# HGRN and GLA level scores: one product for two heads, keys stacked, late queries laid out block-wise with zeros, one pick a level

## The chip, the cores and the metric

The kernel runs on one core of a Trainium2 chip. The metric is the time of one execution on the device in microseconds. The kernel before has a median of 2030.61 us over three runs.

## The reference, cut to what matters

Two layers are computed on 512 tokens of width 1024, all in float32. Each layer has a mixer with four branches, a cross attention and a squared-ReLU MLP. Two of the mixer's branches, HGRN and GLA, are gated linear recurrences with four heads each, worked out in chunks of 64 tokens:

```
def chunk_gated_linear(q, k, v, log_g):
    qc, kc, vc, gc = [jnp.moveaxis(to_chunks(t), 2, 0) for t in (q, k, v, log_g)]
    g_cum = jnp.cumsum(gc, axis=-2)
    def step(s_st, inp):
        ...
        diff = gb[:, :, :, None, :] - gb[:, :, None, :, :]
        decay = jnp.exp(jnp.where(causal[:, :, None], diff, -jnp.inf))
        att = jnp.einsum('bhtk,bhsk,bhtsk->bhts', qb, kb, decay)
        o = o_inter + jnp.einsum('bhts,bhsv->bhtv', att, vb)
```

The head width `dk` is 64 in HGRN and 32 in GLA. The change is in how `att` is computed. The decay between a query t and a key s depends on the channel, so it can't be put on the finished score.

## The kernel before, in words

All activations lie with channels on partitions and the 512 tokens on the free axis. HGRN's queries and keys fill two tiles of 128x512 (heads 0 and 1 in the first, 2 and 3 in the second; `m.J` is 2), GLA's fill one (four heads of 32 partitions; `m.J` is 1). There are 8 chunks (`NCH`) of 64 tokens (`CH`).

The scores of a chunk are made in seven levels. Level 0 is the diagonal s = t. For the levels 1 to 6, with widths w = 32, 16, 8, 4, 2, 1 (`LEVELS`), a chunk is cut into pairs of blocks of w tokens: the keys are those of the early block of a pair, the queries those of the late one, and both are decayed to the border between the blocks. One level is a chain over three engines and back:

- VectorE: `level_diff` subtracts the cumulated log gates from those at the border, for the early and for the late half (two tensor_tensor into `m.E`).
- ScalarE: `level_exp` takes the exponential of `m.E`, and counts up `hg_exp` or `gl_exp`.
- VectorE: `level_mul` multiplies `m.E` into the keys (early half) and into the queries (late half). Both results go to the same tile `m.X`. It counts up `x_ready` (`hg_x`, `gl_x`).
- TensorE: `scores` waits for `x_ready` and runs 32 products, one for each of the 4 heads and 8 chunks. Stationary are 64 keys (64 or 32 partitions), moving are 32 late queries. The chunk's parity picks the lower or the upper 64 partitions of the result. It counts up `lev_done`.
- VectorE: `pick` copies, under a mask, what belongs to this level from PSUM (the banks `M[0]` to `M[3]`) into `m.att` (copy_predicated: 2 a level in HGRN, 4 in GLA), and counts up `picked`.

Each engine works through its own list, written out by hand. TensorE's list is mostly large products: `gemm` and `parts` multiply by weights that come in 680 units of 2 x 256 columns through a ring of 9. For each unit, SyncE's queue loads `w_raw`, ScalarE rounds it to `w_hi` (`feed`, line 1190), and GpSimd subtracts to give `w_lo` (lines 598 and 599), which counts up `split_ready`. TensorE waits for that before a unit. The level scores stand between these blocks: `scores(hg, 3)`, say, stands between the products of the blocks `r_g` and `gate3_0`, and `scores(gl, 6)` ahead of `branch3_2`.

ScalarE feeds units only at certain places of its own list. The five units that start with that of `branch3_2` are fed in `gate(3, 2)`, behind four tanh that wait for `conv(0)` to `conv(3)` on VectorE. VectorE's list there is `level_mul(gl, 3)`, `level_mul(gl, 4)`, two `level_diff`, `pick(gl, 3)`, `merge(3, 0)`, `conv(0)`, `conv(1)`, `pick(gl, 4)`, `level_mul(gl, 5)`, `level_mul(gl, 6)`, `last_decay`, `conv(2)`, `pick(gl, 5)`, `decayed`, `conv(3)`.

Nearly every VectorE and TensorE operation is recorded under the line of a helper: 605 is every matmul, 1660 tensor_tensor, 1669 scalar_tensor_tensor.

Of the kernel before, what the change touches and what calls it, by code (L numbers as in the profile page):

```python
# [19 lines left out]
CH = 64  # L20
# [48 lines left out]
def shape_constants():  # L69
# [27 lines left out]
    put("parity", np.stack([(r // 16) % 2 == 0, (r // 16) % 2 == 1], 1).astype(np.float32))  # L97
    m = np.zeros((P, len(LEVELS), CH), np.int32)
# [54 lines left out]
def is_last(u):  # L153
# [24 lines left out]
    th_used=38, hg_diff=13, s5_prm=1, hg_picked=14, hg_x=6, hg_kdecay_ready=1, hg_state_ready=2, y_act=8, y_ready=8,  # L178
    gl_diff=13, gl_picked=28, gl_x=6, mlstm_cv_ready=4, mlstm_v1=3, gl_kdecay_ready=1, gl_state_ready=2,
# [7 lines left out]
def build(nc, ins, out):  # L187
# [7 lines left out]
    with ctx:  # L195
# [64 lines left out]
        M = [ctx.enter_context(nc.psum_tensor(f"mix{b}", [P, 512], F32)) for b in range(4)]  # L260
# [41 lines left out]
        class Mixer:  # L302


            def __init__(self, pre, tiles, dk, q, k, v, g, gr, e, xx, att, kt, state, o, sq, gscale, oscale, norm):
# [6 lines left out]
                self.X = [Rf(xx + tiles * i, tiles) for i in range(2)]  # L312
# [14 lines left out]
            def score_bank(self, level, h):  # L327
                return M[2 * (level % 2) + h % 2] if self.J == 2 else M[h]

            def score_cols(self, h):  # L330
                return (h // 2) * 256 if self.J == 2 else 0

            def slot(self, h):

                return (h % 2) * 2 + h // 2 if self.J == 2 else h

        hg = Mixer("hg", 2, HD, 4, 2, 6, 0, 8, 10, 14, 18, 20, 22, 10, 12, 1.0, 0.5, "hgrn_norm")
        gl = Mixer("gl", 1, GDK, 26, 27, 28, 32, 30, 10, 12, 14, 20, 22, 12, 10, 1.0 / 16.0, GDK ** -0.5, "gla_norm")
# [264 lines left out]
        def _(pe):  # L603
# [81 lines left out]
            def scores(m, l):  # L685
# [9 lines left out]
                if m.J == 2 and l >= 2:  # L695
                    pe.wait_ge(*of_layer(m.picked, 2 * (l - 1)))
                if m.J == 1 and l >= 1:
                    pe.wait_ge(*of_layer(m.picked, 4 * l))
                kk, qq = (m.K, m.Q) if l == 0 else (m.X[l % 2], m.X[l % 2])

                n = CH if l == 0 else CH // 2
                for h in range(4):
                    rows = slice(m.dk * (h % m.per), m.dk * (h % m.per) + m.dk)
                    base = (h // m.per) * SEQ
                    for c in range(NCH):
                        at_ = m.score_cols(h) + (c // 2) * CH
                        tok = slice(base + c * CH, base + c * CH + CH)
                        late = qq[rows, tok]
                        if l:
                            late = late.rearrange("p (n a c) -> p n a c", a=2, c=LEVELS[l])[:, :, 1, :]  # L710
                        i = mm(m.score_bank(l, h)[64 * (c % 2):64 * (c % 2) + 64, at_:at_ + n], kk[rows, tok], late)
                i.then_inc(m.lev_done, 1)

            def decayed_keys(m):

                pe.wait_ge(*of_layer(m.kd_ready, 1))
                pe.wait_ge(*of_layer(m.picked, 2 * 7 if m.J == 2 else 4 * 7))
# [18 lines left out]
            def outputs(m):  # L736
# [441 lines left out]
        def _(act):  # L1178
# [162 lines left out]
            for L in range(DEPTH):  # L1341
# [25 lines left out]
                do(act.activation(hg.X[1], hg.X[1], ACT.Abs))  # L1367
                do(act.activation(hg.X[1], hg.X[1], ACT.Exp, scale=-1.0))
                do(act.activation(hg.X[1], hg.X[1], ACT.Ln, bias=one), hg.gate_in)
# [287 lines left out]
        def _(dve):  # L1657
# [81 lines left out]
            def level_mul(m, l):  # L1739
# [5 lines left out]
                e, xx, k, q = v(m.E[l % 2]), v(m.X[l % 2]), v(m.K), v(m.Q)  # L1745
                tt(xx[:, :, 0, :], e[:, :, 0, :], k[:, :, 0, :], ALU.mult)
                tt(xx[:, :, 1, :], e[:, :, 1, :], q[:, :, 1, :], ALU.mult, m.x_ready)

            def pick(m, l):

                dve.wait_ge(*of_layer(m.lev_done, l + 1))
                nb = 2 if m.J == 2 else 4
                w = 1024 // nb
                for b in range(nb):
                    bank = m.score_bank(l, b)
                    r = lambda ap: ap.rearrange("p (n c) -> p n c", c=CH)
                    if l == 0:
                        do(dve.copy_predicated(r(m.att[:, b * w:(b + 1) * w]), bc(LM[:, l, :], 1, w // CH), r(bank[:, 0:w])), m.picked)
                        continue
                    dst = m.att[:, b * w:(b + 1) * w].rearrange("p (n s a c) -> p n s a c", n=w // CH, a=2, c=LEVELS[l])[:, :, :, 1, :]  # L1760
                    src = r(bank[:, 0:w])[:, :, 0:CH // 2].rearrange("p n (s c) -> p n s c", c=LEVELS[l])
                    mask = LM[:, l, :].rearrange("p (s a c) -> p s a c", a=2, c=LEVELS[l])[:, :, 1, :]
                    do(dve.copy_predicated(dst, bc(mask, 1, w // CH), src), m.picked)
# [625 lines left out]
```

## Time and profile before

| what | us |
|---|---|
| the three runs | 2030.36, 2030.61, 2031.58 |
| span of the profiled execution, first to last instruction | 2028.1 |
| TensorE matmuls busy | 1999.2 |
| VectorE busy | 961.2 |
| ScalarE busy | 913.2 |
| GpSimd busy | 1062.4 |

The runs lie 2.3 to 3.5 us above the span of the profile, which leaves out what comes ahead of the first and behind the last instruction. A float32 product appears as two matmul records, so that a block of 32 products has 64 of them. A matmul's own duration contains the way through the array. How fast products follow each other is seen from their starts.

### The profile page before, as it was taken

The numbers are of one execution on the slowest core, as the hardware profiler recorded it, in microseconds if no ns is written. First come the engines' busy times: TensorE is split into PE (matmuls) and PEld (weight loads), VectorE is DVE, ScalarE is ACT, GpSimd is POOL, SyncE is SP. The second block draws the span as 40 slices with busy tenths as digits, with TensorE's granted clock in tenths as the row PEclk, the third lists the DMA queues.
The fourth block names the chain that finished last, engine by engine and source line by source line (L and its number), as shares of the span: only waits on it lengthen the run. The fifth ranks groups of instructions, "written<-read, shape, count | busy, mean of one in ns | idle before, by whom it ended". The sixth has DMA issues, their size and how long they took to land. (4 is left out here: it accounts for less than half of the span.)

```text
span 2028.1 us, 32997 instructions
## 1 busy us (share of the span) xinstructions
PE 1999.2 (99%) x12983; PEld 1667.4 (82%) x12983; DVE 961.2 (47%) x1448; ACT 913.2 (45%) x1561; POOL 1062.4 (52%) x1364
## 2 busy tenths in 40 slices
PE   7999999999999999999999999999999999999998
PEld 7788888878998888888897888878788888888887
DVE  6665799845234321211257567997541532211112
ACT  6744554334545542423356536243454544433323
POOL 4564453746744555546466435457377355546451
PEclk9999999999999999999999999999999999999999
DMA  5422233323432333333333232323334233333332
GB/s 176 113 76 76 74 84 86 93 89 94 144 101 68 95 98 99 94 99 97 96 85 90 73 80 79 79 76 97 99 121 129 69 90 97 95 98 99 94 99 73
DMA packets 202678, 191.24 MB, mean 94 GB/s; under 512 B 25658, under 2 KB 200220, under 8 KB 202140
## 3 DMA queue, kind: packets, MB, share of 16 engines
q1 hardware_dynamic: 202524, 189.15, 32.1%
q8 instruction: 102, 1.67, 0.3%
q14 instruction: 52, 0.43, 0.1%
HBM read 184.90 MB, written 3.15 MB: 93 GB/s over the span
## 5 line engine op out<-in xcount | busy, mean ns | idle before, releaser
L598 POOL TENSOR_TENSOR w_lo<-w_raw,w_hi 128x256 fp32r<-128x256 f32 (+1 forms) x680 | 554.2, 815 | 938.2 <-ACT w_hi L1190 937.9
L605 PE MATMUL gemm<-work_split,w_hi 128*128 128x512 f32 (+1 forms) x2048 | 599.6, 377 | 1.8 <-POOL w_lo L599 1.7
L605 PE MATMUL gemm<-h_hi,w_hi 128*128 128x512 f32 (+1 forms) x1456 | 575.9, 396 | 2.3 <-POOL w_lo L599 2.3
L605 PE MATMUL gemm<-h_lo,w_hi 128*128 128x512 f32 (+1 forms) x1456 | 567.3, 390 | 0.0
L605 PE MATMUL gemm<-h_hi,w_lo 128*128 128x512 f32 (+1 forms) x1456 | 567.0, 389 | 0.0
L599 POOL TENSOR_TENSOR w_lo<-w_raw,w_hi 128x256 fp32r<-128x256 f32 (+1 forms) x680 | 557.9, 821 | 0.0
L1190 ACT ACTIVATE w_hi<-w_raw 128x512 fp32r<-128x512 f32 (+1 forms) x680 | 384.0, 619 | 237.7 <-DMA w_raw<-in_mlp_w_dram 185.9
L605 PEld LDWEIGHTS gemm<-work_split,w_hi 128*128 128x128 f32 x2048 | 375.3, 188 | 73.3 <-issue 2.5
L605 PE MATMUL gemm<-work_split,w_lo 128*128 128x512 f32 (+1 forms) x1024 | 384.9, 376 | 0.0
L605 PEld LDWEIGHTS gemm<-h_hi,w_hi 128*128 128x128 f32 (+1 forms) x1456 | 272.7, 187 | 66.0 <-issue 4.2
L605 PEld LDWEIGHTS gemm<-h_hi,w_lo 128*128 128x128 f32 (+1 forms) x1456 | 272.7, 187 | 58.4
L605 PEld LDWEIGHTS gemm<-h_lo,w_hi 128*128 128x128 f32 (+1 forms) x1456 | 272.8, 187 | 57.3 <-issue 1.9
L1660 DVE TENSOR_TENSOR x_t<-x_t,gemm 128x512 f32<-128x512 f32 x96 | 66.0, 688 | 364.0 <-PE gemm L605 363.1
L605 PEld LDWEIGHTS gemm<-work_split,w_lo 128*128 128x128 f32 x1024 | 192.8, 188 | 34.9
L1660 DVE TENSOR_TENSOR work<-work 128x512 f32<-128x512 f32 (+5 forms) x154 | 129.0, 837 | 43.4 <-ACT work L1281 29.3
L1669 DVE SCALAR_TENSOR_TENSOR gate_t<-gemm,work 128x512 f32<-128x512 f32 x64 | 44.3, 692 | 184.3 <-PE gemm L605 167.4
L1635 ACT ACTIVATE gate_t<-gate_t 128x512 f32<-128x512 f32 x64 | 40.5, 632 | 191.0 <-DVE gate_t L1669 191.0
L605 PEld LDWEIGHTS mix<-work 64*64 64x64 f32 (+5 forms) x3776 | 102.1, 130 | 27.2 <-issue 23.8
L605 PE MATMUL mix<-work 64*64 64x64 f32 (+8 forms) x3776 | 121.4, 231 | 0.0
L1275 ACT ACTIVATE gate_t<-gemm 128x512 f32<-128x512 f32 x52 | 31.1, 598 | 131.6 <-PE gemm L605 121.8
L605 PE MATMUL gemm<-w_hi,work_split 128*128 128x256 f32 x384 | 84.8, 288 | 4.3 <-DVE merged_split L1669 2.8
L1669 DVE SCALAR_TENSOR_TENSOR work_split<-gate_t,work_split 128x512 fp32r<-128x512 f32 x64 | 44.7, 699 | 89.0 <-ACT work_split L1636 89.0
(302 smaller groups left out, 1743.7 us busy)
## 6 DMA issues: line engine op xcount, KB each, us to landing
w_raw<-in_mlp_w_dram SPq DMA_DIRECT2D x256, 256.0 KB, 2.7
w_raw<-in_w_in_dram SPq DMA_DIRECT2D x224, 256.0 KB, 2.8
w_raw<-in_xattn_w_kv_dram SPq DMA_DIRECT2D x64, 256.0 KB, 2.8
w_raw<-in_w_branch_dram SPq DMA_DIRECT2D x32, 256.0 KB, 2.7
w_raw<-in_w_out_dram SPq DMA_DIRECT2D x32, 256.0 KB, 2.7
w_raw<-in_xattn_w_q_dram SPq DMA_DIRECT2D x32, 256.0 KB, 2.8
w_raw<-in_xattn_w_o_dram SPq DMA_DIRECT2D x32, 256.0 KB, 2.7
work<-in_x_dram SPq DMA_DIRECT2D x4, 512.0 KB, 6.5
```

Source lines behind the costliest of these rows:

```text
L598: pool.tensor_tensor(lo[:, 0:half], raw[:, 0:half], hi[:, 0:half].bitcast(F32), ALU.subtract)
L599: pool.tensor_tensor(lo[:, half:], raw[:, half:], hi[:, half:].bitcast(F32), ALU.subtract).then_inc(split_ready, 1)
L605: return pe.matmul(o, w, a, start=start, stop=stop, skip_group_check=True)
L1190: act.activation(hi, raw, ACT.Copy).then_inc(split_hi, 1)
L1275: do(act.activation(t[:, b, :], G[s][b][:, :], ACT.Tanh, scale=0.5), th_ready)
L1635: do(act.activation(UPX[1], UPX[0], ACT.Square), up_a)
L1660: do(dve.tensor_tensor(o, a, b, op), s)
L1669: do(dve.scalar_tensor_tensor(out=o, in0=a, scalar=sc, in1=b, op0=op0, op1=op1), s)
```

## The change

Both levels' operands get tiles of their own: `m.early` holds the decayed keys, `m.late` the decayed queries. `m.late` has, for each chunk, 64 columns: 32 late queries times the constant `in_pair` of head 0 of a pair (1 on that head's partitions, 0 on the other's), then the same 32 times that of head 1. One product of stacked keys (128 partitions in HGRN, 64 in GLA) with these 64 columns gives the scores of two heads beside each other. So `scores` has 16 products a level for level 1 to 6 where there were 32. `pick` becomes one copy_predicated of 512 columns a level from level 1 on; for GLA it reads over two banks. `level_mul` becomes three operations: one for the keys and, for each head of a pair, one scalar_tensor_tensor for the queries. In HGRN's levels 1 and 2 the one for the keys takes all 1024 columns. Level 0 stays as it was but for where it writes in `m.att`. The banks go round differently: HGRN uses one of four a level, GLA two of four, and TensorE's waits for `picked` reach further back.

```diff
@@ class Mixer
-            def score_bank(self, level, h):
-                return M[2 * (level % 2) + h % 2] if self.J == 2 else M[h]
+            def score_bank(self, level):
+                return (level + 1) % 4 if self.J == 2 else 2 - 2 * (level % 2)
@@ scores
-                if m.J == 2 and l >= 2:
-                    pe.wait_ge(*of_layer(m.picked, 2 * (l - 1)))
-                if m.J == 1 and l >= 1:
-                    pe.wait_ge(*of_layer(m.picked, 4 * l))
-                kk, qq = (m.K, m.Q) if l == 0 else (m.X[l % 2], m.X[l % 2])
-
-                n = CH if l == 0 else CH // 2
-                for h in range(4):
-                    rows = slice(m.dk * (h % m.per), m.dk * (h % m.per) + m.dk)
-                    base = (h // m.per) * SEQ
...
+                elif m.J == 2:
+                    if l >= 3:
+                        pe.wait_ge(*of_layer(m.picked, max(2, l - 2)))
+                    for j in range(2):
+                        for c in range(NCH):
+                            o = M[m.score_bank(l)][64 * (c % 2):64 * (c % 2) + 64, (j * 4 + c // 2) * CH:(j * 4 + c // 2 + 1) * CH]
+                            i = mm(o, m.early[l % 2][:, (j * NCH + c) * CH:(j * NCH + c + 1) * CH], m.late[l % 2][:, (j * NCH + c) * CH:(j * NCH + c + 1) * CH])
+                else:
+                    pe.wait_ge(*of_layer(m.picked, max(4, l + 2)))
                     for c in range(NCH):
...
+                        for p in range(2):
+                            rows = slice(64 * p, 64 * p + 64)
+                            o = M[m.score_bank(l) + p][64 * (c % 2):64 * (c % 2) + 64, (c // 2) * P:(c // 2 + 1) * P]
+                            i = mm(o.rearrange("p (h x) -> p h x", h=2)[:, :, 0:CH // 2], m.early[l % 2][rows, c * CH:(c + 1) * CH],
+                                   m.late[l % 2][rows, c * CH:(c + 1) * CH])
@@ level_mul
-                e, xx, k, q = v(m.E[l % 2]), v(m.X[l % 2]), v(m.K), v(m.Q)
-                tt(xx[:, :, 0, :], e[:, :, 0, :], k[:, :, 0, :], ALU.mult)
-                tt(xx[:, :, 1, :], e[:, :, 1, :], q[:, :, 1, :], ALU.mult, m.x_ready)
+                e, k, q = v(m.E[l % 2]), v(m.K), v(m.Q)
+                if m.J == 2 and l <= 2:
+                    tt(m.early[l % 2], m.E[l % 2], m.K, ALU.mult)
+                else:
+                    tt(v(m.early[l % 2])[:, :, 0, :], e[:, :, 0, :], k[:, :, 0, :], ALU.mult)
+                of_chunk = lambda ap: ap.rearrange("p (n s) c -> p n s c", s=CH // (2 * w))
+                late = m.late[l % 2].rearrange("p (n h s c) -> p n h s c", h=2, s=CH // (2 * w), c=w)
+                for h in range(2):
+                    stt(late[:, :, h, :, :], of_chunk(e[:, :, 1, :]), m.in_pair[:, h:h + 1], of_chunk(q[:, :, 1, :]), ALU.mult, ALU.mult,
+                        m.x_ready if h else None)
@@ pick, levels 1 to 6
+                dst = m.att.rearrange("p (n s a c) -> p n s a c", n=16, a=2, c=w)[:, :, :, 1, :]
+                if m.J == 2:
+                    src = M[m.score_bank(l)].rearrange("p (n c) -> p n c", n=16)
+                else:
+                    b = m.score_bank(l)
+                    src = MIX[:, 512 * b:512 * b + 1024].rearrange("p (n c) -> p n c", n=16)[:, :, 0:CH // 2]
+                mask = LM[:, l, :].rearrange("p (s a c) -> p s a c", a=2, c=w)[:, :, 1, :]
+                do(dve.copy_predicated(dst, bc(mask, 1, 16), src.rearrange("p n (s c) -> p n s c", c=w)), m.picked)
```

VectorE, from `pick(hg, 1)` to `level_mul(hg, 3)` and `pick(hg, 2)`, before:

```order
L1763 COPY_PREDICATED work<-masks_sb,mix 128x8x32 [waits hg_scores,vector_steps]
L1763 COPY_PREDICATED work<-masks_sb,mix 128x8x32 [waits hg_picked]
L1660 TENSOR_TENSOR work<-work 128x128x4 [waits hg_x,hg_picked]
L1660 TENSOR_TENSOR work<-work 128x128x4 [waits hg_diff]
L1669 SCALAR_TENSOR_TENSOR work<-gate_t,gemm 128x512 [waits th_ready,hg_diff]
L1669 SCALAR_TENSOR_TENSOR work<-gate_t,gemm 128x512 [waits th_used,th_ready]
L1660 TENSOR_TENSOR work<-work 128x64x8 [waits th_used,hg_scores,hg_exp]
L1660 TENSOR_TENSOR work<-work 128x64x8 [waits vector_steps]
L1763 COPY_PREDICATED work<-masks_sb,mix 128x16x16 [waits hg_scores,hg_x]
L1763 COPY_PREDICATED work<-masks_sb,mix 128x16x16 [waits hg_picked]
```

and the same stretch of VectorE now:

```order
L1785 COPY_PREDICATED work<-masks_sb,mix 128x16x32 [waits hg_scores,vector_steps]
L1669 TENSOR_TENSOR work<-work 128x128x4 [waits hg_x,hg_picked]
L1669 TENSOR_TENSOR work<-work 128x128x4 [waits hg_diff]
L1678 SCALAR_TENSOR_TENSOR work<-gate_t,gemm 128x512 [waits th_ready,hg_diff]
L1678 SCALAR_TENSOR_TENSOR work<-gate_t,gemm 128x512 [waits th_used,th_ready]
L1669 TENSOR_TENSOR work<-work 128x64x8 [waits th_used,hg_scores,hg_exp]
L1678 SCALAR_TENSOR_TENSOR work<-work,consts_sb 128x16x32 [waits vector_steps] x2
L1785 COPY_PREDICATED work<-masks_sb,mix 128x32x16 [waits hg_scores,hg_x]
```

The order of the steps is the same; each pick is one row instead of two, and the second tensor_tensor of a `level_mul` has become two scalar_tensor_tensor. Ahead of this stretch, `level_mul(hg, 1)` and `level_mul(hg, 2)` on VectorE are now:

```order
L1669 TENSOR_TENSOR work<-work 128x1024 [waits hg_exp,pro_tensor,hg_picked]
L1678 SCALAR_TENSOR_TENSOR work<-work,consts_sb 128x16x32 [waits vector_steps] x2
L1669 TENSOR_TENSOR work<-work 128x1024 [waits hg_exp,hg_x]
L1678 SCALAR_TENSOR_TENSOR work<-work,consts_sb 128x16x32 [waits vector_steps] x2
L1669 TENSOR_TENSOR work<-work 128x64x8 [waits hg_x]
```

where there were four tensor_tensor of 512 columns; the last row is the first of `level_diff(hg, 3)`, which follows as before.

## Rows read from the trace of the kernel before

**Rows 1.** The page: busy us (share); a group's busy us, mean ns of one.

```profile
PE 1999.2 (99%) x12983; PEld 1667.4 (82%) x12983; DVE 961.2 (47%) x1448; ACT 913.2 (45%) x1561; POOL 1062.4 (52%) x1364
...
L605 PE MATMUL mix<-work 64*64 64x64 f32 (+8 forms) x3776 | 121.4, 231 | 0.0
```

**Rows 2.** TensorE's waits: total us, times, longest us.

```profile
PE gemm L605 <- POOL w_lo L599: 5.5, 6, 1.5
```

**Rows 3.** TensorE's timeline around `scores(hg, 3)`, layer 1, then layer 2: start, us.

```profile
113.43 0.39 PE L605 MATMUL gemm<-h_hi,w_lo 128*128 128x512 f32 x1
113.75 1.46 PE L605 MATMUL mix<-work 64*64 64x32 f32 x64
...
1109.65 1.46 PE L605 MATMUL mix<-work 64*64 64x32 f32 x64
```

**Rows 4.** TensorE's timeline: blocks of other shapes.

```profile
150.06 2.79 PE L605 MATMUL mix<-work 64*64 64x64 f32 x120
...
360.05 0.86 PE L605 MATMUL mix<-work 128*32 128x32 f32 x64
...
366.52 3.71 PE L605 MATMUL mix<-work 128*64 128x128 f32 x64
```

**Rows 5.** TensorE's timeline: `scores(hg, 1)`, `scores(gl, 1)`, `scores(gl, 3)`, first of `branch3_2`.

```profile
99.64 1.46 PE L605 MATMUL mix<-work 64*64 64x32 f32 x64
...
170.53 1.45 PE L605 MATMUL mix<-work 32*64 32x32 f32 x64
...
190.21 1.45 PE L605 MATMUL mix<-work 32*64 32x32 f32 x64
...
220.90 0.50 PE L605 MATMUL gemm<-work_split,w_hi 128*128 128x512 f32 x1
```

**Rows 6.** VectorE's timeline in HGRN's levels.

```profile
96.69 5.58 DVE L1660 TENSOR_TENSOR work<-work 128x512 f32<-128x512 f32 x6 [5.14 <-ACT work L1281]
...
105.13 0.93 DVE L1763 COPY_PREDICATED work<-masks_sb,mix 128x256 f32<-128x256 int32 x2
...
109.79 1.84 DVE L1660 TENSOR_TENSOR work<-work 128x512 f32<-128x512 f32 x2 [0.22 <-DVE work L1669]
...
129.43 1.52 DVE L1763 COPY_PREDICATED work<-masks_sb,mix 128x256 f32<-128x256 int32 x2 [1.68 <-PE mix L605]
```

**Rows 7.** GpSimd's timeline: its first and last operation beside that stretch.

```profile
98.42 1.01 POOL L598 TENSOR_TENSOR w_lo<-w_raw,w_hi 128x256 fp32r<-128x256 f32 x1 [8.43 <-ACT w_hi L1190]
...
106.29 1.17 POOL L599 TENSOR_TENSOR w_lo<-w_raw,w_hi 128x256 fp32r<-128x256 f32 x1
```

**Rows 8.** VectorE's timeline, single operations: prices by width, alone and beside GpSimd.

```profile
97.42 0.69 DVE L1660 TENSOR_TENSOR work<-work 128x512 f32<-128x512 f32 x1
...
110.52 1.12 DVE L1660 TENSOR_TENSOR work<-work 128x512 f32<-128x512 f32 x1
...
126.11 1.64 DVE L1660 TENSOR_TENSOR work<-work 128x1024 f32<-128x1024 f32 x1
...
130.99 1.23 DVE L1660 TENSOR_TENSOR work<-work 128x1024 f32<-128x1024 f32 x1
...
158.15 0.75 DVE L1669 SCALAR_TENSOR_TENSOR work<-work,params_all 128x512 f32<-128x512 f32 x1 [9.33 <-ACT work L1308]
```

**Rows 9.** VectorE's timeline in GLA's levels.

```profile
168.88 0.85 DVE L1660 TENSOR_TENSOR work<-work 128x256 f32<-128x256 f32 x1
...
189.04 3.65 DVE L1660 TENSOR_TENSOR work<-work 128x256 f32<-128x256 f32 x8 [5.72 <-ACT work L1281]
192.72 1.30 DVE L1763 COPY_PREDICATED work<-masks_sb,mix 128x128 f32<-128x128 int32 x4
...
211.32 1.90 DVE L1763 COPY_PREDICATED work<-masks_sb,mix 128x128 f32<-128x128 int32 x4 [0.17 <-PE mix L605]
```

**Rows 10.** The unit of `branch3_2`: ScalarE's last tanh, GpSimd's second half.

```profile
216.97 0.63 ACT L1449 ACTIVATE work<-work 128x512 f32<-128x512 f32 x1 [5.11 <-DVE work L1669]
...
219.05 1.17 POOL L599 TENSOR_TENSOR w_lo<-w_raw,w_hi 128x256 fp32r<-128x256 f32 x1
```

More of the change, by code:

```diff
@@ L97, in shape_constants @@
     put("parity", np.stack([(r // 16) % 2 == 0, (r // 16) % 2 == 1], 1).astype(np.float32))
+    put("in_pair", np.stack([(r // w) % 2 == n for w in (64, 32) for n in range(2)], 1).astype(np.float32))
     m = np.zeros((P, len(LEVELS), CH), np.int32)
@@ L259, in build @@
         G = [[ctx.enter_context(nc.psum_tensor(f"gemm{s}{b}", [P, 512], F32)) for b in range(2)] for s in range(2)]
-        M = [ctx.enter_context(nc.psum_tensor(f"mix{b}", [P, 512], F32)) for b in range(4)]
+        MIX = ctx.enter_context(nc.psum_tensor("mix", [P, 4 * 512], F32))
+        M = [MIX[:, 512 * b:512 * b + 512] for b in range(4)]
         def bc(ap, axis, n):
@@ L302, in build, with __init__ @@
         class Mixer:
-            def __init__(self, pre, tiles, dk, q, k, v, g, gr, e, xx, att, kt, state, o, sq, gscale, oscale, norm):
+            def __init__(self, pre, tiles, dk, q, k, v, g, gr, e, xx, early, att, kt, state, o, sq, gscale, oscale, norm):
                 self.pre, self.J, self.dk, self.gscale, self.oscale, self.norm = pre, tiles, dk, gscale, oscale, norm
@@ L311, in __init__ @@
                 self.E = [Rf(e + tiles * i, tiles) for i in range(2)]
-                self.X = [Rf(xx + tiles * i, tiles) for i in range(2)]
+                self.late = [Rf(xx + tiles * i, tiles) for i in range(2)]
+                self.early = [Rf(early + 2 * i, tiles) for i in range(2)]
+                self.in_pair = const("in_pair")[:, 0:2] if tiles == 2 else const("in_pair")[:, 2:4]
                 self.att = Rf(att, 2)
@@ L725, in state_in @@
                 pe.wait_ge(*of_layer(m.kt_ready, m.J))
+                pe.wait_ge(*of_layer(m.picked, 8 if m.J == 2 else 10))
                 pe.wait_ge(*of_layer(values_ready, VALUES_AT[m.pre]))
@@ L1366, in _ @@
                        hg.kq_ready if j else None)
-                do(act.activation(hg.X[1], hg.X[1], ACT.Abs))
-                do(act.activation(hg.X[1], hg.X[1], ACT.Exp, scale=-1.0))
-                do(act.activation(hg.X[1], hg.X[1], ACT.Ln, bias=one), hg.gate_in)
+                do(act.activation(hg.late[1], hg.late[1], ACT.Abs))
+                do(act.activation(hg.late[1], hg.late[1], ACT.Exp, scale=-1.0))
+                do(act.activation(hg.late[1], hg.late[1], ACT.Ln, bias=one), hg.gate_in)
                 feed_past("r_q")
@@ L1753, in pick @@
[L1753 to L1763, printed above, removed]
+                if l == 0:
+                    att = m.att.rearrange("p (j t h c) -> p j t h c", j=2, t=TT, h=2)
+                    for b in range(2 if m.J == 2 else 4):
+                        if m.J == 2:
+                            dst, n = att[:, :, :, b, :].rearrange("p j t c -> p (j t) c"), 8
+                        else:
+                            dst, n = att[:, b // 2, :, b % 2, :], 4
+                        do(dve.copy_predicated(dst, bc(LM[:, l, :], 1, n), M[b][:, 0:n * CH].rearrange("p (n c) -> p n c", c=CH)), m.picked)
+                    return
```

43 lines of the change are left out of this document (24 added, 19 removed).

## The prediction

> **What bounds the kernel now.** The page comes first: TensorE is busy for 1999.2 us of the span, 99% of it, and no other engine for more than 52% [rows 1]. Its waits come next: the longest group is 5.5 us in six waits for `w_lo` [rows 2]. So the kernel is bound by what TensorE has to do in its own order, and a level's scores are part of that. The third view is TensorE's timeline at a score block. The last large product starts at 113.43, the block at 113.75, after the 0.32 that every such block shows. The block lasts 1.46 for 64 records (32 products, two records each), in the second layer just the same [rows 3]. Without the last record's own 0.23 [rows 1], the starts take 1.23 us, 20 ns a record. GLA's blocks last 1.45 [rows 5]. There are 24 such blocks (six levels, two branches, two layers) and none of them waits for VectorE. The fourth view is VectorE's timeline there, which tells how near the operands come. All depends on it, because the change gives VectorE more to do ahead of the blocks.
>
> **TensorE, removed.** A block now has 32 records instead of 64. No row has a 128*64 product with 64 moving columns. The same stationary shape with 128 columns starts a record every (3.71 - 0.23) / 63 = 55.2 ns [rows 4]. If columns set it, 64 of them take 27.6 ns, and 31 intervals with 0.05 for the start give 0.90 us. If they don't, it is 55.2 x 31 = 1.71. The quickest small shape, 128*32 with 32 columns, starts one every (0.86 - 0.23) / 63 = 10 ns [rows 4], which gives 0.31. I take 0.90, since that shape differs in one number only: HGRN saves 0.33 a level, 4.0 us in 12. For GLA (64*64, 64 columns, row halves and column halves in turn) the nearest row is the block of 120 records in 2.79 [rows 4], 21.5 ns a record, of which about half go round four quarters of the array and the rest round two. At 27 ns for the latter, the former take about 16 ns, so 31 intervals take 0.50 (between 0.31 and 0.67). GLA, whose block takes 1.22 now, saves 0.72 a level, 8.6 us in 12. Together that is 12.6 us of TensorE's work.
>
> The Trainium skill ("TensorE: Matmul & The Clock Gate", section "Back-to-back issue gap") says that 1 to 64 moving columns cost the same, some 25 ns a matmul. The trace has 20 ns a record here, and by this rule 32 records take 0.8 in both branches and save 0.43 a level, 10.3 us in all.
>
> **VectorE, added.** Prices: a tensor_tensor of 512 columns takes 0.69 alone and 1.12 while GpSimd works on `w_lo`; one of 1024 takes 1.23 alone and 1.64 beside it. A scalar_tensor_tensor of 512 with a per-partition factor takes 0.75 alone [rows 8], and I take 1.12 beside GpSimd. Between two operations lie 0.035. A pick costs 0.465 for 256 columns and 0.325 for 128, so 0.74 for 512; in the levels w = 2 and 1 it is 0.76 for 256 and 0.475 for 128, so 1.36 for 512 [rows 6, 9].
>
> **HGRN.** VectorE works without a break from 96.69 to 109.79 [rows 6], with GpSimd beside it from 98.42 to 107.46 in eight operations [rows 7]. Before, `hg_x` for level 1 came at 98.11, 1.53 ahead of the block at 99.64 [rows 5, 8]. Now it comes at 96.69 + 1.265 + 0.785 + 1.12 = 99.86: the block waits about 0.3. Level 2's multiplications end at 99.90 + 1.675 + 1.155 + 1.12 = 103.85 instead of about 99.98 (four tensor_tensor from 96.69, three alone and one beside GpSimd). From there to `level_mul(hg, 3)` there were 9.81 us. The pick gives back 0.19, and I take off 0.5, since `level_diff(hg, 4)` now falls into GpSimd's pause. So it starts at 112.95 and takes 0.725 + 1.155 + 1.12 = 3.0: `hg_x` comes at 115.95, where it came at 111.63 for a block at 113.75 [rows 3, 6]. TensorE would be there at 113.75 + 0.3 - 2 x 0.33 = 113.4 and waits 2.7 (with 0.1 from the count to the first product). Behind the waiting product stand the large ones of `gate3_0` and all of TensorE's list, so the wait is paid in full. What is late next: level 4 needs a pick (0.77), `level_diff(hg, 5)` and three multiplications, at most 0.77 + 2.3 + 3.4 = 6.5 after level 3, and the next block comes 7.05 - 0.33 = 6.7 after it (7.05 is half of the way from 99.64 to 113.75). That is just in time, and so is level 5. The later operations fall into pauses that VectorE had (1.68 ahead of the pick at 129.43 [rows 6]). ScalarE feeds units some us later there; none of today's waits for `w_lo` is long (six in all, the longest 1.5 [rows 2]). In a layer HGRN gives 6 x 0.33 - 3.0 = -1.0 us.
>
> The bounds of this wait: with the added operations alone on the port they cost 1.4 + 1.4 + 0.8 - 0.2 = 3.4 instead of 4.3, and the two waits are 2.1. With GpSimd beside each of them they cost 6.0, and the waits are 4.7.
>
> **GLA.** A `level_mul` grows from 0.91 to 0.465 + 2 x 0.515 = 1.50. Level 1's second operation ended at 168.88 + 0.85 = 169.73 [rows 9], ahead of a block at 170.53 [rows 5]. Now the end is at about 170.6: a wait of 0.15. Level 2 has more room. Level 3's multiplications start at 189.04, when ScalarE's exponential is ready, and ended 0.91 later for a block at 190.21 [rows 5, 9]; now they end at 190.50, a wait of 0.35. For the levels 4 to 6 the operands are early by more than that.
>
> The costlier wait is at `branch3_2`. ScalarE's tanh at 216.97 waited for `conv(3)` on VectorE. Only behind it does ScalarE feed the unit of `branch3_2`, and GpSimd ends its second half at 219.05 + 1.17 = 220.22 [rows 10], for products that began at 220.90 [rows 5]. That is 0.7 to spare on one chain: VectorE from 189.04 on, which has hardly a pause up to `conv(3)`. Along this chain the change adds four `level_mul` (4 x 0.585 = 2.34), takes off 1.34 - 0.77 = 0.57 at each of `pick(gl, 3)` and `pick(gl, 4)` and 1.93 - 1.36 = 0.57 at `pick(gl, 5)`, and uses up the 0.17 that VectorE stood idle there for TensorE [rows 9]. The sum is +0.46: the unit is ready at 220.7. But TensorE, with four blocks shortened, would be there at 220.90 - 4 x 0.72 + 0.35 = 218.4. It waits 2.4, and from the start of level 3 to `branch3_2` it gains 0.15 instead of 2.88. Afterwards units come in time, and both engines' lists are as before. In a layer GLA gives 2 x 0.72 - 0.15 + 0.15 = +1.44 us.
>
> Bounds: with the factors' operations at tensor_tensor's price (0.43), the chain is not longer at all and the gain is 0.6 instead of 0.15. With one operation of each `level_mul` beside GpSimd (+0.4 each) it is 2.1 longer and 1.5 are lost.
>
> Costless: four more constant columns, the wait of `level_mul(hg, 1)` for the prologue's transposes (long done by then), other addresses in `m.att`, and the waits for `picked`, which reach further back.
>
> **The sum.** 2 x (1.44 - 1.0) = 0.9 us off the span of 2028.1, so 2027.2. The median of the runs is 2.5 above the span: 2029.7.
>
> **Rivals.** (A) The forecast: most of the 12.6 us turns into waits. 0.55; its own range is 2026.9 (both lower bounds: -0.1 and +1.9 a layer) to 2032.5.
> (B) The waits don't come and TensorE's saving is the result: 2030.6 - 12.6 = 2018.0. For it: 99% busy and no wait for VectorE today [rows 1, 2]. Against it: margins of 1.53, 2.1, 0.8, 0.26 and 0.7 us against more than 4 us of added work. 0.08.
> (C) Only one of the two long waits comes. Without `branch3_2`'s, 2 x 2.4 more are gained: 2024.9. Without HGRN's, 2 x 3.0: 2023.7. Both sums rest on several prices, so 0.12.
> (D) Slower: GpSimd stands beside each added operation. The added work ahead of `hg_x` for level 3 is then 6.0 instead of 4.3, and the waits in HGRN come to 4.7; in GLA the chain grows by 2.1. That is a layer at -2.7 - 0.2, 5.8 in both: 2036.4. It decides once the two chains together are longer by 2.6 a layer than I take. For it: GpSimd follows ScalarE's feeding, which VectorE's delay also moves. Against it: GpSimd has a fixed number of operations and its pauses stay. 0.12, of which most is over 2034.7.
> (E) VectorE and GpSimd shut each other out for a whole operation: 0.69 + 0.73 = 1.42 instead of the 1.12 of [rows 8], 0.3 more for each of four added operations, 1.2 a layer: 2032.0. 0.05. The Trainium skill states this rule ("SBUF — State Buffer", section "Terms": the port pair is locked for the whole instruction and the loser "fully blocks"). The trace speaks against the full price here.
> (F) A block is quicker or slower than taken. In levels 1 to 3 of HGRN and 3 to 6 of GLA a wait swallows it, so it moves the time by under 2 us: 0.08.
>
> **How the numbers follow.** 0.2% is 4.1 us, about what a measurement can tell from no change. Faster means under 2026.5: B, C and a little of A and F, 0.22. Slower means over 2034.7: most of D, 0.12. Within it 0.66. The range takes in C from below and part of D: 2023.5 to 2035.0.
>
> **What the profile will show.** HGRN's blocks at about 0.9 and GLA's at 0.5 from first to last start; TensorE waiting for VectorE about 2.7 at `scores(hg, 3)` and 0.3 at `scores(hg, 1)`; about 2.4 for GpSimd's `w_lo` at `branch3_2`; TensorE's busy time down by about 12.6 and its waits up by 12. If waits at these places are missing, B or C holds; if the one in HGRN is over 4, D.

## The result, and the profile after

The changed kernel takes 2034.24 us (median of 20 runs, 2032.16 to 2036.66). The kernel before takes 2031.12 in 20 runs (2029.70 to 2032.49). The ratio is 1.0017, with a 95% interval of 1.0011 to 1.0023: slower by some 3 us, where the forecast was 0.9 us faster. The profiled execution has a span of 2032.3 us; its whole time is 1.8 us more.

Two lines of the page, as in [rows 1]:

```profile
PE 1993.9 (98%) x12215; PEld 1660.3 (82%) x12215; DVE 976.3 (48%) x1424; ACT 912.6 (45%) x1561; POOL 1067.3 (53%) x1364
...
L606 PE MATMUL mix<-work 64*64 64x64 f32 (+7 forms) x3008 | 109.1, 235 | 5.9 <-DVE work L1678 5.9
```

And TensorE's waits, as in [rows 2] (total us, times, longest us):

```profile
PE gemm L606 <- POOL w_lo L600: 9.2, 7, 2.4
PE mix L606 <- DVE work L1678: 5.9, 6, 2.4
```

The waits that were forecast have come: 5.9 us for VectorE's scalar_tensor_tensor (L1678) in six waits, where there were none, and 9.2 us for `w_lo` instead of 5.5. But TensorE's busy time fell by 5.3 us only, while its group of small products fell by 12.3 (from 121.4 [rows 1]). So the rest of its work, which the change doesn't touch, is busy for 7 us more. That is the first sign. TensorE's timeline of blocks gives their sizes (start, us, and in brackets the idle time before it). The rows are `scores(hg, 1)`, `(hg, 3)` and `(hg, 4)` in layer 1, `scores(gl, 1)` and `(gl, 3)`, then `(hg, 3)` and `(hg, 4)` in layer 2:

```profile
100.56 1.15 PE L606 MATMUL mix<-work 128*64 128x64 f32 x32 [0.30 <-DVE work L1678]
...
116.50 1.52 PE L606 MATMUL mix<-work 128*64 128x64 f32 x32 [2.37 <-DVE work L1678]
124.79 1.15 PE L606 MATMUL mix<-work 128*64 128x64 f32 x32
...
173.70 0.69 PE L606 MATMUL mix<-work 64*64 64x64 f32 x32
192.23 0.69 PE L606 MATMUL mix<-work 64*64 64x64 f32 x32 [0.28 <-DVE work L1678]
...
1115.33 1.15 PE L606 MATMUL mix<-work 128*64 128x64 f32 x32 [2.38 <-DVE work L1678]
1122.07 1.15 PE L606 MATMUL mix<-work 128*64 128x64 f32 x32
```

A block of HGRN takes 1.15 and one of GLA 0.69, where each took 1.46 or 1.45 [rows 3, 5]. The two blocks `(hg, 3)` had waited equally long, 2.37 and 2.38. Yet from the one to `(hg, 4)` it is 8.29 us in layer 1 and 6.74 in layer 2, with the same instructions between. The large products in between show why. Timeline of TensorE in layer 1, directly behind the block:

```profile
117.96 0.80 PE L606 MATMUL gemm<-h_hi,w_hi 128*128 128x512 f32 x1
118.55 0.63 PE L606 MATMUL gemm<-h_lo,w_hi 128*128 128x512 f32 x1
118.98 0.63 PE L606 MATMUL gemm<-h_hi,w_lo 128*128 128x512 f32 x1
...
119.83 0.63 PE L606 MATMUL gemm<-h_lo,w_hi 128*128 128x512 f32 x1
120.26 0.51 PE L606 MATMUL gemm<-h_hi,w_lo 128*128 128x512 f32 x1
120.61 0.40 PE L606 MATMUL gemm<-h_hi,w_hi 128*128 128x512 f32 x1
120.84 0.39 PE L606 MATMUL gemm<-h_lo,w_hi 128*128 128x512 f32 x1
```

From 118.55 to 120.26 they start 0.43 us apart, and 0.23 apart from 120.61 on. The windows say what that is. The columns are us; busy us of PE, PEld, DVE, ACT and POOL; PEclk, the granted clock; the DMA share; GB/s. First come four rows of layer 1 at `scores(hg, 3)` and two at `branch3_2`, then two and one of layer 2 at the same places:

```profile
114.00:116.00 2.00, 0.14 (x1) 0.00 (x0) 1.93 (x3) 1.97 (x5) 2.00 (x3) 1.00 0.36 79
116.00:118.00 2.00, 1.50 (x33) 1.38 (x33) 1.93 (x3) 0.20 (x1) 2.00 (x3) 0.77 0.15 52
118.00:120.00 2.00, 2.00 (x7) 1.62 (x6) 1.93 (x3) 0.49 (x1) 2.00 (x3) 0.50 0.00 0
120.00:122.00 2.00, 2.00 (x10) 1.62 (x9) 1.93 (x3) 0.57 (x1) 2.00 (x3) 0.87 0.00 0
222.00:224.00 2.00, 1.61 (x5) 1.36 (x6) 1.97 (x2) 1.46 (x3) 2.00 (x3) 0.73 0.00 0
224.00:226.00 2.00, 2.00 (x6) 1.52 (x6) 1.93 (x3) 0.00 (x0) 2.00 (x4) 0.50 0.00 0
...
1116.00:1118.00 2.00, 2.00 (x25) 1.67 (x20) 1.93 (x3) 0.00 (x0) 2.00 (x3) 1.00 0.00 0
1118.00:1120.00 2.00, 2.00 (x11) 1.65 (x10) 1.93 (x3) 1.06 (x1) 2.00 (x3) 1.00 0.00 0
1220.00:1222.00 2.00, 2.00 (x6) 1.52 (x6) 1.93 (x3) 0.70 (x2) 2.00 (x4) 0.50 0.00 0
```

Behind three of the four waits of 2.4 us the granted clock is 0.50, the lower of its two levels (1.2 instead of 2.4 GHz), for some us, and TensorE issues 6 or 7 products in 2 us instead of 10 or 11. Nothing of this is idle time: in the page it counts as busy, which is why the busy time hardly fell. At `branch3_2` the wait is the one forecast and the price is the same:

```profile
1219.62 1.19 PE L606 MATMUL gemm<-work_split,w_hi 128*128 128x512 f32 x2 [2.42 <-POOL w_lo L600]
...
1224.04 0.60 PE L728 MATMUL mix<-consts_sb,work 128*128 128x128 f32 x4
```

Its twelve large products take 4.42 us from the first start to the next group. In the kernel before they took 2.86 (from 220.90 [rows 5] to 223.76). So each fall costs about 1.55: 8.29 - 6.74 at `scores(hg, 3)`, 4.42 - 2.86 at `branch3_2`. Three of them are 4.65 us. With the forecast's -0.9 that is +3.8, and this execution's span has grown by 4.2.

The sum can be made without the forecast. From level 0 of HGRN to the block behind `branch3_2` TensorE falls behind the kernel before by 2.48 us in layer 1 and by 0.86 in layer 2, 3.3 together: 4.65 for the clock and -1.3 for the change itself. The rest isn't the change's work. Some 0.54 us were lost ahead of 86 us, where nothing had changed yet, and 0.5 by a wait for `w_lo` near 340 us, 1.12 where it was 0.63.

The Trainium skill ("TensorE: Matmul & The Clock Gate", section "Back-to-back issue gap") says that at 1.2 GHz lone products start columns divided by the clock apart. By this formula the estimate for 512 columns is 427 ns. The trace agrees: 0.43. The same page (section "HAM oscillation — how this bites in real kernels") describes waits that send the array to the lower clock, so that the work behind them starts there. The forecast did not weigh that rule.

### The profile page after: what moved, and what is told of

Same layout as the page of the kernel before. It is cut to its first block and busy times, and to the rows that moved or that the text cites. A ratio compares the mean times of both kernels' runs of the same rounds, so it can differ in the third digit from the quotient of the medians.

```text
span 2032.3 us, 31435 instructions
## 1 busy us (share of the span) xinstructions
PE 1993.9 (98%) x12215; PEld 1660.3 (82%) x12215; DVE 976.3 (48%) x1424; ACT 912.6 (45%) x1561; POOL 1067.3 (53%) x1364
## 5 line engine op out<-in xcount | busy, mean ns | idle before, releaser
L1669 DVE TENSOR_TENSOR work<-work 128x512 f32<-128x512 f32 (+5 forms) x130 | 112.8, 868 | 43.0 <-ACT work L1290 29.7
L1678 DVE SCALAR_TENSOR_TENSOR gate_t<-gemm,work 128x512 f32<-128x512 f32 x64 | 44.3, 692 | 184.7 <-PE gemm L606 167.9
L606 PEld LDWEIGHTS mix<-work 64*64 64x64 f32 (+5 forms) x3008 | 89.1, 131 | 33.6 <-issue 22.2
L606 PE MATMUL mix<-work 64*64 64x64 f32 (+7 forms) x3008 | 109.1, 235 | 5.9 <-DVE work L1678 5.9
L1678 DVE SCALAR_TENSOR_TENSOR work_split<-gate_t,work_split 128x512 fp32r<-128x512 f32 x64 | 44.7, 699 | 88.9 <-ACT work_split L1645 88.9
```

The source lines that it names most:

```text
L606: return pe.matmul(o, w, a, start=start, stop=stop, skip_group_check=True)
L1669: do(dve.tensor_tensor(o, a, b, op), s)
L1678: do(dve.scalar_tensor_tensor(out=o, in0=a, scalar=sc, in1=b, op0=op0, op1=op1), s)
```

## The experiments

Two theories stood at the start. **K**: the forecast's waits are right in place and length, and what it lacks is the half clock behind them. **L**: what it lacks is length, more waiting or later operands somewhere, and the clock is a companion. Each time is a median of runs on one chip beside the kernel before (2030.7 to 2030.9 there). The interval of such a ratio is some 1.8 us to either side for 11 runs, so the times alone often can't tell K from L, and the traces have to.

**1. `fill`: the same waits, but TensorE isn't idle in them.**

```diff
+                    if m.J == 2 and l == 3:
+                        pe.wait_ge(*of_layer(m.picked, 2))
+                        for _ in range(10):
+                            mm(M[m.score_bank(l)], Hhi[:, 0, 0:P], Hhi[:, 0, :])
                     pe.wait_ge(*of_layer(m.x_ready, l))
...
+                if name == "branch3_2":
+                    for _ in range(10):
+                        mm(G[s][0][:, 0:n], Hhi[:, 0, 0:P], Hhi[:, 0, :])
```

> The changed kernel, with ten products of 512 columns (0.23 us each, 2.3 us in all) that TensorE carries out ahead of its wait at scores(hg, 3) and ahead of its wait at branch3_2; their results are overwritten by the first product behind the wait. Nothing else changes, so the large products behind a wait can begin no earlier than they did. Theory K (clock): the 2.4 us in which TensorE stood still are followed by a stretch at half the clock, which costs about 1.5 us each time and is what the forecast lacks. Here TensorE isn't idle, the granted clock stays at 1.00 in 118 to 122 us and in 223 to 226 us, and the time falls from 2034.2 by 3 to 6 us, to 2028 to 2031. Rival L (length): the forecast lacks something in the waits themselves or elsewhere (late operands, VectorE's added work, transfers), and the clock is only a companion. Then the time stays at 2034, or rises if the ten products delay what stands behind them.

Measured: 2030.76 us in 11 runs, 0.9999 of before (0.9991 to 1.0008). The timeline of `fill` has the ten products in the place of the wait. The block starts 9.22 us behind the start of `scores(hg, 2)`, in the changed kernel 9.18, so it comes no earlier in its stretch:

```profile
113.50 2.43 PE L606 MATMUL mix<-h_hi 128*128 128x512 f32 x10
116.06 1.15 PE L606 MATMUL mix<-work 128*64 128x64 f32 x32
122.80 1.15 PE L606 MATMUL mix<-work 128*64 128x64 f32 x32
```

The next block follows after 6.74 and not 8.29. The windows show the clock at 1.00 there, and at `branch3_2` (same columns):

```profile
118.00:120.00 2.00, 2.00 (x11) 1.64 (x10) 1.97 (x2) 0.92 (x1) 2.00 (x3) 1.00 0.00 0
...
222.00:224.00 2.00, 2.00 (x12) 1.63 (x11) 1.93 (x3) 0.00 (x0) 2.00 (x4) 1.00 0.00 0
```

Twenty useless products in a layer take off 3.5 us. At `branch3_2` the ten had themselves to wait for a bank (0.70 and 0.64), and the useful ones began 0.69 and 0.61 us later behind the start of `scores(gl, 6)` than in the changed kernel. So useful work began no earlier anywhere, and L could not give the 3.5. K holds. Together with the 1.3 of added delay it is 4.8, about three falls of 1.55. The time is no different from before; the forecast's -0.9 lies within the interval too.

**2. `feed` and `later`: each wait taken away by itself.** In `feed` ScalarE feeds the unit of `branch3_2` ahead of its fourth tanh:

```diff
                 for j in range(4):
+                    if j == 3:
+                        feed(first_unit("branch3_2") + 1)
                     act.wait_ge(*of_layer(ms["cv_ready"], j + 1))
```

> The changed kernel, with ScalarE feeding the unit of branch3_2 ahead of the last of its four tanhs (the one that waits for conv(3)) and not behind it. If the unit's wait is what the chain through conv(3) makes of it, the 2.4 us at branch3_2 vanish in both layers. Theory K: with them goes the half clock behind them, 1.5 us each: 2034.2 - 2 x 3.9 = 2026.4. Rival L: only the length comes back, 2034.2 - 4.8 = 2029.4. Rival M (moved): VectorE's chain is as late as before, and TensorE now waits at decayed_keys(gl) or state_in(gl) instead: 2033 to 2034.

In `later` HGRN's blocks stand further back in TensorE's list:

```diff
                 rest(block)
-                scores(hg, 3)
                 block = gate_parts(3, 0)
-                some(block, 2)
+                some(block, 1)
+                scores(hg, 3)
+                some(block, 2)
                 scores(hg, 4)
                 rest(block)
-                scores(hg, 5)
                 block = parts("m_q", *H)
+                some(block, 1)
+                scores(hg, 5)
                 some(block, 2)
                 scores(hg, 6)
-                some(block, 1)
+                rest(block)
                 decayed_keys(hg)
-                rest(block)
```

> The changed kernel, with scores(hg, 3), (hg, 4) and (hg, 5) one unit (3.3 us) later in TensorE's list, and scores(hg, 6) and decayed_keys(hg) one part later. hg_x for level 3 came 2.4 us too late, so the wait should vanish; the later levels have as much time between them as before. Theory K: 2 x 2.4 and the half clock in one layer of two (1.5 us), 2034.2 - 6.3 = 2027.9. Rival L: 2034.2 - 4.8 = 2029.4. Rival M: VectorE does level 4 only behind level 3's block, so that the wait comes back at a later level: 2032 to 2034.

Measured: `feed` 2030.49 (0.9996, 0.9987 to 1.0005), `later` 2028.40 (0.9988, 0.9979 to 0.9997). For `feed`, K's 2026.4 was missed by 4.1, and L's 2029.4 by 1.1. The unit now came in time, but behind that wait stood another, for the bank that VectorE frees with `merge(3, 1)`:

```profile
1216.70 0.73 PE L606 MATMUL gemm<-work_split,w_hi 128*128 128x512 f32 x2 [1.35 <-DVEq L1728]
...
1218.00:1220.00 2.00, 2.00 (x13) 1.67 (x11) 1.97 (x2) 0.93 (x2) 2.00 (x3) 1.00 0.01 4
```

The wait is 1.35 in both layers, with no fall behind either. With this wait in the sum, K gives 2034.2 - 2 x (1.06 + 1.55) = 2029.0 and L 2032.1. The measured 2030.5 lies between, 1.5 us from either, so `feed` doesn't decide. In its profiled execution the clock holds behind `scores(hg, 3)` in layer 1 and falls in layer 2, the other way round than in the changed kernel, behind equal waits.

`later` has no wait at `scores(hg, 3)`, but a new one of 0.94 at `state_in(hg)` for ScalarE's copies (I had put `decayed_keys(hg)` with no part of `m_q` behind it). It is 5.8 us under the changed kernel. The length gives only 2 x (2.4 - 0.94) = 2.9, and one fall with it 4.5. That it lies within 0.5 of K's 2027.9 is luck in part, because that figure had no new wait in it. It is well over what L has.

**3. `both`: the two edits.**

> The changed kernel with both edits: ScalarE feeds the unit of branch3_2 ahead of the fourth tanh, and HGRN's scores stand one unit later. Theory K: no wait of over 1 us is left at these places and the clock stays at 1.00, so that TensorE's saving of 12.6 us is nearly whole: 2018.0 and the small waits that stay (0.37, 0.1, 0.35 a layer, 1.6 in all), 2019.6. Rival L: 2034.2 - 9.6 = 2024.6. Rival M, the waits moved: over 2028.

Measured: 2025.00 in 7 runs (0.9973, 0.9962 to 0.9984). That is within 0.4 us of the sum of the two single gains, and 5.4 over K's 2019.6: the waits of 1.33 or 1.35 and of 0.94 in each layer are 4.6 of it. L's 2024.6 was met, but it had no waits left in it: with the 4.6 in the sum it would be 2029.2. K's 2019.6 with them is 2024.2. In this execution the clock is at 1.00 from 40 us to the last 4.

**4. `hg_alone` and `gl_alone`: one part of the change at a time.** The other branch keeps its scores, multiplications, picks and layout of before, as in this piece of `scores` for `hg_alone`:

```diff
+                if m.J == 1:
+                    if m.J == 1 and l >= 1:
+                        pe.wait_ge(*of_layer(m.picked, 4 * l))
+                    kk, qq = (m.K, m.Q) if l == 0 else (m.late[l % 2], m.late[l % 2])
...
-                if l == 0:
+                elif l == 0:
```

> HGRN's levels as in the changed kernel, GLA's scores, multiplications, picks and layout as before. Theory K: 12 blocks save 0.3 each (3.6 us), the waits at scores(hg, 1) and scores(hg, 3) cost 2 x (0.37 + 2.4) = 5.5, and the half clock behind the longer one 1.6 in at least one layer: 2030.8 - 3.6 + 5.5 + 1.6 = 2034.3, so that HGRN's part alone makes the kernel slower. Without a cost of the clock (rival L): 2032.7. If the two parts hinder each other and neither alone is late: 2027.

> GLA's levels as in the changed kernel, HGRN's scores, multiplications, picks and layout as before; level_mul(gl, 1) and (gl, 2) write all columns of their early operand (0.26 us more each). Theory K: 12 blocks save 0.74 each (8.9 us), the waits at scores(gl, 1), (gl, 3) and branch3_2 cost 2 x (0.35 + 0.35 + 2.4) = 6.2, the half clock behind branch3_2's 2 x 1.5: 2030.8 - 8.9 + 6.2 + 3.0 = 2031.1. Rival L: 2028.1. If branch3_2 is late only through HGRN's delay, it does not wait here: 2023.

Measured: `hg_alone` 2034.46 (1.0018, 1.0009 to 1.0027) against K's 2034.3 and L's 2032.7; `gl_alone` 2030.88 (0.9998, 0.9990 to 1.0007) against 2031.1 and 2028.1. For `gl_alone` L lies outside the interval; for `hg_alone` the two theories are too close for the times to tell. K's 2034.3 had one fall in it. The profiled execution of `hg_alone` has one in each layer, which makes it 2035.9 by the same sum, and it took 2035.93. HGRN's part is the one that loses: its blocks give 0.31 each, and its wait with the half clock costs more. GLA's gives 0.76 a block, 9.1 in 12, and loses 7.9 of it at `branch3_2` (4.8 of waiting and two falls). Windows of `gl_alone` behind that wait, layers 1 and 2:

```profile
222.00:224.00 2.00, 2.00 (x6) 1.58 (x5) 1.83 (x3) 0.00 (x0) 2.00 (x3) 0.50 0.00 0
1218.00:1220.00 2.00, 2.00 (x7) 1.59 (x6) 1.93 (x3) 0.12 (x1) 2.00 (x3) 0.53 0.00 0
```

**5. `light`: VectorE's added work taken away.** One of the two scalar_tensor_tensor operations of each `level_mul` is left out, so that half of the late queries aren't written, and the scores of one head in two are others. TensorE's products stay the same in number and shape.

```diff
-                for h in range(2):
+                for h in (1,):
```

> The changed kernel without the first of the two scalar_tensor_tensor operations of every level_mul: the half of the late queries that belongs to the first head of a pair isn't written (the scores of one head in two are therefore others), while TensorE's products stay the same in number and shape. It takes some 0.5 to 1.1 us off VectorE ahead of each block. If VectorE's added operations are what TensorE waits for (theories K and L alike), hg_x for level 3 comes by 112.9 and the unit of branch3_2 by about 218.5, the waits of 2.4 us shrink to under 0.6, no stretch at half the clock is left, and the saving of 12.6 us shows almost whole: 2018 to 2020. If the waits have another cause (TensorE's shorter blocks bringing it ahead of ScalarE's feeding): over 2026.

Measured: 2020.58 in 5 runs (0.9948, 0.9935 to 0.9962). There is no wait at `scores(hg, 3)`, one of 0.68 at `branch3_2`, and the clock is 0.998 over the span. So VectorE's operations are what TensorE waits for. TensorE's own saving of 12.8 us is real: less 1.4 of waits, 11.4 were to be seen and 10.4 are, within the interval.

**6. `stall3`, `stall4`, `stall6`: waits of three lengths in the kernel before.** They have nothing of the change in them. The diff is that of `stall3`; the others have 4 and 6 in the place of the 3.

```diff
-                tt(xx[:, :, 0, :], e[:, :, 0, :], k[:, :, 0, :], ALU.mult)
+                for _ in range(1 + 3 * (m.J == 2 and l == 3)):
+                    tt(xx[:, :, 0, :], e[:, :, 0, :], k[:, :, 0, :], ALU.mult)
```

> The kernel before the change, in which VectorE carries out the first multiplication of level_mul(hg, 3) four times and not once (the same numbers into the same place; three added operations of 1.12 beside GpSimd, 3.46 us). The operands were 2.1 us early, so TensorE waits some 1.4 us at scores(hg, 3), in both layers. It separates a wait's length from what the clock does behind it, in a kernel without the change. Theory K: waits of 1.35 us left the clock at 1.00 in earlier runs, so only the length counts: 2030.9 + 2 x 1.4 = 2033.7. Rival L: the same. If the half clock follows any wait here: 2036.8.

> The kernel before the change with that multiplication carried out five times (4.62 us added): a wait of some 2.5 us at scores(hg, 3) in both layers. Theory K: the half clock stands behind it in one layer or both, 1.5 us each: 2030.9 + 5.0 + 1.5 to 3 = 2037.4 to 2038.9, and a spread of the runs of some 3 us. Rival L (only the length, or the half clock belongs to the change's own products): 2035.9 and the spread of before.

> The kernel before the change with that multiplication carried out seven times (6.93 us added): a wait of some 4.8 us at scores(hg, 3) in both layers. Theory K: the half clock stands behind it in both layers; the loss beyond the length is 1.5 to 2 us each, as behind 2.4 us, or more: 2030.9 + 9.6 + 3 to 4 = 2043.5 to 2044.5. Rival L: 2040.5.

Measured: 2036.08 (2033.98 to 2038.72), 2039.31 (2038.78 to 2039.63) and 2045.92 (2044.90 to 2047.36) beside 2030.67 for before. The blocks `(hg, 3)` and `(hg, 4)` of both layers, first in `stall3`:

```profile
114.89 1.46 PE L605 MATMUL mix<-work 64*64 64x32 f32 x64 [1.27 <-DVE work L1660]
121.95 1.46 PE L605 MATMUL mix<-work 64*64 64x32 f32 x64
...
1112.95 1.46 PE L605 MATMUL mix<-work 64*64 64x32 f32 x64 [1.26 <-DVE work L1660]
1121.62 1.46 PE L605 MATMUL mix<-work 64*64 64x32 f32 x64
```

Then layer 1 of `stall4`, layer 1 of `stall6`, and two windows of `stall6` with the clock behind its wait:

```profile
117.10 1.66 PE L605 MATMUL mix<-work 64*64 64x32 f32 x64 [2.40 <-DVE work L1660]
125.72 1.46 PE L605 MATMUL mix<-work 64*64 64x32 f32 x64
```

```profile
118.74 2.44 PE L605 MATMUL mix<-work 64*64 64x32 f32 x64 [4.66 <-DVE work L1660]
128.40 1.46 PE L605 MATMUL mix<-work 64*64 64x32 f32 x64
```

```profile
118.00:120.00 2.00, 1.26 (x38) 1.26 (x40) 1.90 (x4) 0.00 (x0) 1.27 (x2) 0.50 0.04 8
...
122.00:124.00 2.00, 2.00 (x6) 1.52 (x6) 1.90 (x4) 0.23 (x1) 0.00 (x0) 0.50 0.00 0
```

Between the blocks lie 7.05 us when the clock holds. `stall3` has 7.06 and 8.67 behind waits of the same length, `stall4` 8.62 and 8.59, `stall6` 9.66 and 9.57. So a fall costs 1.55 to 1.6 behind 1.3 or 2.4 us of standing still and 2.5 to 2.6 behind 4.7, where the lower clock lasts twice as long. `stall4` adds up: 2 x 2.40 + 2 x 1.55 = 7.9 of the 8.6 measured; `stall6` 2 x 4.66 + 2 x 2.6 = 14.5 of 15.2. `stall3` was expected at 2033.7 by both theories and is 2.4 over it. Its profiled execution, 2034.98, has one fall. None, one or two falls of 1.6 would put an execution at some 2033.4, 2035.0 or 2036.6. Five of the eight runs lie in this range. The three longest (2037.3 to 2038.7), which also have the lowest clock, 0.995, lie 0.7 to 2.1 above it, and that stays unexplained. The condition that I had read from `feed` (waits of 1.35 leave the clock alone) was wrong. The effect itself has nothing to do with the change's products.

**7. `best` and `best2`: what the change is worth.** On `both`: one part of `m_q` stands behind `decayed_keys(hg)` again, ScalarE feeds up to four units ahead of its fourth tanh, and VectorE frees the bank first:

```diff
-                rest(block)
                 decayed_keys(hg)
+                rest(block)
...
-                        feed(first_unit("branch3_2") + 1)
+                        feed(first_unit("branch3_2") + 4)
...
-                conv(3)
                 merge(3, 1)
+                conv(3)
```

> The kernel with both edits, and three more: decayed_keys(hg) directly behind scores(hg, 6) and the last part of m_q behind it; ScalarE feeds four units (not one) ahead of its fourth tanh; VectorE does merge(3, 1) ahead of conv(3). In the kernel with both edits TensorE still waited 1.33 at branch3_2 for VectorE's merge(3, 1) and 0.94 at state_in(hg) for ScalarE's copies, in each layer. If these waits only sit in a bad order: 2025.0 - 2 x (1.2 + 0.6) = 2021.4. If VectorE's chain is the bound from scores(gl, 3) to state_in(gl), the wait moves to decayed_keys(gl) or outputs(gl): 2024 to 2025.

Measured: 2023.62 (0.9962, 0.9950 to 0.9975), 2.2 over the 2021.4 that was expected if the waits only sat in a bad order. The wait at `state_in(hg)` is gone. The one at `branch3_2` is gone as well, but 1.02 and 1.06 us of it stand now at the next block, for banks that ScalarE frees behind the tanh that waits for `conv(3)`. Hence `best2`, with ScalarE's `gate(3, 2)` ahead of that tanh:

```diff
                     if j == 3:
-                        feed(first_unit("branch3_2") + 4)
+                        gate(3, 2)
...
-                gate(3, 2)
                 kt_copy(gl)
```

> The best kernel so far, with ScalarE's gate(3, 2) (its feeding included) ahead of its fourth tanh. There TensorE still waited 1.02 and 1.06 us for ScalarE to free the banks of gate3_2, behind the tanh that waits for conv(3). If that is all: 2023.6 - 2.1 = 2021.5. If VectorE's chain through merge(3, 2) is as late: 2023.6.

Measured: 2020.07 in 5 runs (2019.79 to 2021.30), 0.9951 of before (0.9938 to 0.9963), 14 us under the changed kernel and 1.4 under the 2021.5 expected. No run has these moves without the change. But the kernel before has no waits at these places that they could take away, and TensorE's 12.8 us less small waits of 0.3 are enough for the gain. The longest waits that VectorE still causes for a score block are in this line:

```profile
PE mix L606 <- DVE work L1680: 1.1, 4, 0.3
```

## Why the prediction was wrong, point by point

**TensorE's blocks: right.** From the first start to the last 0.93 (1.15 without the last record's 0.22) against 0.90, and 0.48 against 0.50. In 24 blocks 12.8 us against 12.6. The rule of the Trainium skill ("TensorE: Matmul & The Clock Gate", section "Back-to-back issue gap"), 25 ns a matmul whatever its columns up to 64, holds for neither branch: the 32 records start 30 ns apart in HGRN and 15 in GLA. The measurement decides.

**The waits: right in all five places.** Forecast 0.3, 2.7, 0.15, 0.35 and 2.4; in the trace 0.30, 2.37 and 2.38, 0.1, 0.28, and 2.40 and 2.42. From the start of a block to the start of the next, all of them and the small changes at the joints cost 11.5 us in both layers, so that the change would have given 1.3 at the full clock where 0.9 was forecast. The prices behind the waits held too. VectorE's timeline ahead of `scores(hg, 3)` begins 0.56 later than before, as does all of this stretch:

```profile
97.25 1.23 DVE L1669 TENSOR_TENSOR work<-work 128x1024 f32<-128x1024 f32 x1 [5.15 <-ACT work L1290]
98.51 1.90 DVE L1678 SCALAR_TENSOR_TENSOR work<-work,consts_sb 128x512 f32<-128x512 f32 x2
100.44 1.63 DVE L1669 TENSOR_TENSOR work<-work 128x1024 f32<-128x1024 f32 x1
...
109.52 0.74 DVE L1785 COPY_PREDICATED work<-masks_sb,mix 128x512 f32<-128x512 int32 x1
...
114.22 2.23 DVE L1678 SCALAR_TENSOR_TENSOR work<-work,consts_sb 128x512 f32<-128x512 f32 x2
```

The two factors' operations (scalar_tensor_tensor) take 1.9 with one beside GpSimd and 2.23 with both (0.75 + 1.12 and 2 x 1.12 were taken), the pick 0.74. `hg_x` for level 3 comes at 116.45, less 0.56 is 115.89, where 115.95 was forecast.

**The step that failed: "so the wait is paid in full".** A wait of the engine that bounds the kernel was priced at its length, and its length was taken as its whole price. The sum had no term for TensorE's clock. It needed 1.55 us for each long wait behind which the clock falls. With the three of the profiled execution the forecast of 2029.7 would have been 2034.4 against a median of 2034.24. That it fits so closely is chance: the kernel before had a median of 2031.1 and not 2030.6 in the 20 runs, and the number of falls varies. Neither the bounds nor the list of what could make it slower (D and E: dearer VectorE operations) had this mechanism. The trace of the kernel before had one such place, at its start. TensorE's next product stands at 13.50 behind a wait of 2.67 for VectorE, and the granted clock is 0.50 from 14.8 to 18.2 us:

```profile
PE gemm L605 <- DVE merged_split L1669: 2.8, 2, 2.7
...
16.00:18.00 2.00, 2.00 (x11) 2.00 (x11) 1.60 (x4) 1.93 (x4) 1.36 (x2) 0.50 1.09 372
```

The prediction read only the first group of waits and took no window of the clock. Behind 40 us TensorE had no wait over 1.2 us, so that the price of a fall between large products wasn't to be read there.

**The rivals.** A, with its mechanism, is what the trace shows. B (no waits), 2018.0, is nearly `light`, 2020.6. C, one of the two waits only, was thought worth 5 to 6 us; `later`, without HGRN's, gained 5.8, of which the clock is a part. D and E are out, although D's time was also slower than before: VectorE's prices are those of the forecast. F is out, since the blocks are as long as forecast.

**What stays open.** In the profiled executions of all these kernels, behind the first 40 us, 12 of 14 waits of 2.33 to 2.42 us were followed by the half clock, both of 4.66 us, one of six of 1.26 to 1.35, and none of 0.9 to 1.2. What decides it for one wait (the same instruction, layer 1 and not layer 2) no run here tells apart. The first 40 us, in which TensorE often waits, are not in this count. There the lower clock stands once or twice, for 3 to 7 us in all, in every profiled execution but that of `fill`, also behind some waits of 1.4 to 1.8, and not in the same places. The start as a whole differs: TensorE is ready for `scores(hg, 1)` between 99.5 and 101.4 us. Nor are the last 4 to 8 us in the count, where TensorE has nothing left to do and the clock is at 0.50 in all of them.

## What to carry to other kernels

When the engine that bounds a kernel gets less to do, its operands must come earlier by as much. Otherwise the gain turns into waits at the places with the least to spare, and on TensorE a wait of 2.4 us mostly cost another 1.55 in clock, hidden in its busy time. Look at the granted clock behind each long wait ahead of counting the idle time. And the gain was only late, not lost: a few moves in the lists of three engines turned +3.1 us into -10.6.

## What the runs showed of the hardware

A TensorE that stood still for 2.4 us ran 3 to 4 us behind it at 0.50 of its clock in 12 of 14 cases: 512-column products start 0.43 apart instead of 0.23, at 1.55 us a time. Ten products with no use (0.23 each) in the gap at the two places of each layer kept it at 1.00. The fall comes late, mostly only when the products run again: in layer 1 of the changed kernel the window of 114 to 116 us, in which TensorE did nothing, has 1.00, and the one of 118 to 120, in which it was busy throughout, 0.50.
